# A decoder step with the memory keys at the head of its first portion and a gate bias added by VectorE

## The chip, the core and the metric

One core of a Trainium2 chip runs the kernel. The metric is the device time of one execution in microseconds (us). The runs of the kernel before took 2277.1, 2276.29 and 2273.66 us, so the median is 2276.29 us. Everything is float32.

## The reference, cut to what matters

Two layers, each over 256 prompt tokens (two tiles of 128) and 32 sample tokens, width 1024. What the first portion (layer 0, first prompt tile) has to compute, and where the change works:

```python
mem_n = _rmsnorm(mem_prompt, mem_norm_g[l])          # 256 memory tokens
kp = (mem_n @ w_mem_k[l]);  vp = (mem_n @ w_mem_v[l])  # keys and values, both outputs too
h = _rmsnorm(x, norm_mix_g) @ w_in                   # u_a v_a val_b gate_b q_m gl_a gl_b gl_m
s = einsum(tril(ws), layernorm(gelu(v_a))) + bs[:, :L]   # spatial gate, bias per group and token
y_a = gelu(u_a) * s
y_b = silu(layernorm(causal_depthwise(val_b * sigmoid(gate_b), w, b)))   # 31 taps
y_m = softmax(q_m @ kp * HD**-0.5) @ vp              # 4 heads of 256
x = x + (sig(gl_a)*(y_a@w_o_a) + sig(gl_b)*(y_b@w_o_b) + sig(gl_m)*(y_m@w_o_m)) @ w_out
x = x + peer(rmsnorm(x))     # 8 heads, 16 of 16384 experts each, rows fetched from memory
```

A norm of memory token t is a factor of t alone, and the gain a factor of the channel alone. So `mem_n @ W` can be had as `((gain * mem) @ W) * norm[t]`.

## The kernel before, in words

The work is cut into four portions m = 0 to 3: m = 0 and 2 are the first prompt tile of layer 0 and 1 (128 tokens), m = 1 and 3 the second tile with the 32 sample tokens. A portion's dense part is written out for each engine as a generator `mixing(m)`. Portion 0 runs by itself from the start of the kernel; the mixing of every later portion is woven into the expert stage of the portion before, by the tables `parts` and `PLACE`. The expert stage gathers pairs of expert rows with indirect DMAs and needs the scores that portion 0 ends with, so nothing of it runs before portion 0 is over.

Within portion 0 each engine takes its steps strictly in the order of the code. SP loads weights in pieces of 1024 KB into a ring of four buffers (`ring`, L400), in the order of `items(m)`; the load of piece n waits until TensorE has finished piece n-4. At the start SP first loads the token rows x, the constants, `small` (gains and taps) and `vecs`, then four ring pieces, then the memory (L418).

TensorE's pieces have short names. `glu0` to `glu7` are the conv module's gate and value, 16 matmuls of 128 columns each; `mk0` to `mk3` memory keys, 16 of 256 columns; `mv0` to `mv3` memory values, 16 of 256; `q0` to `q3` queries, 16 of 128; `va`, `ua` the spatial gate's v and u; `S`, `T`, `O` are scores, transposes and outputs of one attention head; `gt` and `pr` gate and own projections, 8 matmuls of 512 columns; `sg0` to `sg3` the spatial gate itself. A float32 matmul stands in the trace as two rows, so that a piece of 16 matmuls has x32. Its results go to three PSUM banks in turn (`dense`), and each piece waits until the result three pieces earlier has left its bank.

TensorE begins portion 0 by turning x (L1543, once VectorE has made the diagonal of row norms), then runs glu0 to glu7, mk0 with q0 and so on. The memory is normed in `ext_s` before mk0: ScalarE squares it, VectorE sums (L1021), takes the root's reciprocal and multiplies all eight blocks (L1030).

The depthwise convolution is VectorE's: 62 steps, each four instructions over a half of the channels and one tap (L962, L964). It can start when glu7 has left its bank. `beside(name, taps)` puts a fixed number of steps at a fixed place: 32 of them in the attention stretch, 8 before the first two `pr`, 16 among `ua` and `sg`. Whatever is left is done by `conv(2 * CONV_W)` after sg3. Then VectorE sums the blocks (L1225), TensorE adds over partitions (L1818, `csum`), and only behind that matmul do pr2 and the rest of portion 0 follow on TensorE.

In `spatial` each group's product gets the bias by a second, eight-row matmul (L1807), and VectorE multiplies the sum into u (L1221). With mv0 SP issues two spreads of LayerNorm vectors over all partitions (L446, 512 KB each, into `uv` buffers still free) and four early weight pieces for portion 1 (`EARLY`, L450, 1024 KB each).

Of the kernel before, what the change touches and what calls it, by code (L numbers as in the profile page):

```python
# [50 lines left out]
def items(m):  # L51
    if m % 2 == 0:
# [20 lines left out]
for _k, _c in WKIND:  # L73
# [8 lines left out]
    memsq=(1, 0), pe_memsq=(1, 0), memvar=(1, 0), rt_mem=(1, 0), memn=(8, 0), pe_mk=(4, 0), kt=(4, 0), pe_mv=(4, 0), vm=(4, 0),  # L82
# [28 lines left out]
def parts(p):  # L111
# [15 lines left out]
    out = [("rows", 4), ("tr", 6)] + some("glu", h, *range(8))  # L127
    if p == 0:
# [28 lines left out]
for _p in range(2):  # L157
    _at, _place = 0.0, {}
    for _name, _cost in parts(_p):
        _place[_name] = _at  # L160
        _at += _cost
    _place["end"] = _at
    PLACE.append(_place)
# [5 lines left out]
for _p in range(2):  # L169
# [4 lines left out]
def emptied(m, name):  # L174

    last = TURN[m % 2][name][1]
# [30 lines left out]
def build(nc, x_in, consts_in, mem_in, cache_in, state_in, w_in, small_in, vecs_in, fing_in, ws_in, wss_in,  # L207
          keys_in, uv_in, y_out, memk_out, memv_out, convp_out, convs_out, vn_out):
    with ExitStack() as ctx:
# [17 lines left out]
        spread_landed = sem("spread_landed")  # L227
        conv_stored, vn_stored, y_stored = sem("conv_stored"), sem("vn_stored"), sem("y_stored")
# [23 lines left out]
        ln_rows = [uvbuf[i][:, 0:D] for i in range(2)]  # L252

# [102 lines left out]
        def dense(m, name):  # L356
            return turn[TURN[m % 2][name][0] % 3]
# [13 lines left out]
        def _(sp):  # L371
            def load(m, kind, i):
                if (m, kind, i) in EARLY:
                    return
# [26 lines left out]

            sp.dma_start(x[:, 0], x_in[:, 0]).then_inc(x_landed[0], 16)
            sp.dma_start(consts[:, :], consts_in).then_inc(consts_landed, 16)
            for m in range(PORTIONS):
# [9 lines left out]
                for n, it in enumerate(items(m)):  # L414
                    if p == 0 and n == 4:
                        if m:
                            sp.wait_ge(S["pe_so"], at("pe_so", m, 0))
                        sp.dma_start(ext_s_flat[:, 0:KB * M], mem_in).then_inc(mem_landed, 16)  # L418
                        if m == 0:
# [63 lines left out]
        def _(pool):  # L483
# [27 lines left out]
            def mixing(m):  # L511
                l, p = m // 2, m % 2
                place = PLACE[p]
# [42 lines left out]
        def _(act):  # L556
# [18 lines left out]
            def mixing(m):  # L575
                l, p = m // 2, m % 2
                place, nt, tiles = PLACE[p], COLS[p], TB[p]

                yield place["rows"]
                if m != 1:  # L580
                    norm_rows(m)

                for c in range(KB):
# [8 lines left out]
                    if p == 0 and c == 1:  # L592
# [3 lines left out]
                    if p == 0 and c == (4 if m == 0 else 3):  # L596
# [67 lines left out]
                if p == 0:  # L664
# [268 lines left out]
        def _(dve):  # L933
            V = nc.vector

            def norm_rows(m):
                for i, t in enumerate(TB[m % 2]):
# [14 lines left out]
            def mixing(m):  # L952
                l, p = m // 2, m % 2
                place, nt, tiles = PLACE[p], COLS[p], TB[p]
# [45 lines left out]

                for c in range(KB):
# [17 lines left out]
                    if m == 0 and c == 2:  # L1019
                        dve.wait_ge(S["memsq"], 1)  # L1020
                        V.tensor_reduce(rb_mem, kT.rearrange("p c t -> p t c"), AX.X, ALU.add).then_inc(S["memred"], 1)  # L1021
                    if p == 0 and c == (4 if m == 0 else 2):
                        dve.wait_ge(S["pe_memsq"], at("pe_memsq", m, 1))
                        V.tensor_scalar(rb_mem, s_bank[0][:, 0:M], 1.0 / D, EPS, ALU.mult, ALU.add).then_inc(S["memvar"], 1)
                    if p == 0 and c == (5 if m == 0 else 4):
# [38 lines left out]
                if p == 0:  # L1064
# [114 lines left out]
                def norm_v_gain():  # L1179
# [5 lines left out]
                    if m == 0:  # L1185
                        dve.wait_ge(spread_landed, 32)
# [23 lines left out]
                def spatial():  # L1210
                    for i in range(3):
                        yield from beside(f"ua{i}", 2 - p)
                    for i in range(4):
# [6 lines left out]
                        u = yMA[:, 2 * i:2 * i + 2, 0:nt]  # L1220
                        V.tensor_tensor(u, u, two(dense(m, f"sg{i}"), nt), ALU.mult).then_inc(S["ya"], 1)  # L1221
# [218 lines left out]
            dve.wait_ge(consts_landed, 16)  # L1440
# [48 lines left out]
        def _(pe):  # L1489
# [627 lines left out]
```

## Time and profile before

| | |
|---|---|
| median of the runs | 2276.29 us |
| profiled execution, own time | 2276.56 us |
| its span | 2274.8 us |
| TensorE busy over the span | 71% |
| VectorE busy | 69% |
| ScalarE, GpSimd busy | 29% each |
| data moved | 895.53 MB, 394 GB/s on average |
| portion 0's dense part on TensorE | from 6.99 us to about 300 us |

The profiled execution's own time holds some 1.8 us outside its span. The shares are means over the whole kernel; the change touches only the first 200 us, and what counts there is which engine is waited for at which moment. The page's table in 40 slices shows TensorE at 8 to 9 tenths in the first slices of 57 us and the granted clock at 9 of 10 or more in the first seven.

### The profile page before, as it was taken

How to read it: one execution, taken by the hardware profiler on the slowest of the kernel's cores; microseconds unless marked ns; L12 is line 12 of the kernel's file. 1: busy time of each engine (PE TensorE's matmuls, PEld its weight loads, DVE VectorE, ACT ScalarE, POOL GpSimd, SP SyncE). 2: the span in 40 equal slices, each digit the busy share in tenths (PEclk: the TensorE clock that was granted, in tenths of full speed). 3: DMA queues.
4: the chain of work that ended last, by engine and by line, in shares of the span. 5: the costliest groups of instructions: out<-in, count | busy, mean ns of one | idle time of the engine just before them, and what ended most of it. 6: DMA issues, size and time to landing. Idle time of an engine off the chain costs nothing.

```text
span 2274.8 us, 31198 instructions
## 1 busy us (share of the span) xinstructions
PE 1623.5 (71%) x10876; PEld 1051.8 (46%) x10876; DVE 1576.3 (69%) x4199; ACT 662.8 (29%) x1662; POOL 662.1 (29%) x596
## 2 busy tenths in 40 slices
PE   8999977679898567778878656865999853334333
PEld 8865766347775235454533424632878620000001
DVE  3545277877767576877776557977776677776875
ACT  2112234321233232323123223342123333322222
POOL 0000032222233342323223233321223344444442
PEclk9999989779899678889979766986999875555555
DMA  8686789999999999999999999999999999999997
GB/s 305 262 301 240 288 332 422 419 421 422 412 408 419 421 420 421 422 397 419 421 394 415 421 421 403 422 403 421 382 420 421 418 398 422 422 422 421 421 421 308
DMA packets 127099, 895.53 MB, mean 394 GB/s; under 512 B 16064, under 2 KB 16896, under 8 KB 19168
## 3 DMA queue, kind: packets, MB, share of 16 engines
q0 software_dynamic: 83232, 604.02, 64.4%
q1 hardware_dynamic: 43712, 289.53, 31.8%
q8 instruction: 87, 1.43, 0.2%
q14 instruction: 68, 0.56, 0.1%
HBM read 885.38 MB, written 8.11 MB: 393 GB/s over the span
## 4 chain that ended last, share of the span: by engine, by line
PE 35%; DMA 34%; DVE 19%; issue 4%; ACT 4%; DVEq 3%; POOL 2%; another core or an unknown queue 0%; POOLq 0%; ACTq 0%
DMA uv<-uv_in,idx_u 24%; PE bank L1499 15%; DVE uv L1378 9%; PE bank L1754 5%; DMA ring<-w_in 5%; PE bank L1505 5%; PE bank L2006 4%; DMA ring<-cache_in 4%; DVE yB L964 2%; POOL uv L506 2%; ACT L558 1%; ACT diag L881 1%; DVE x L1399 1%; PE bank L1939 1%; DVEq L959 1%
## 5 line engine op out<-in xcount | busy, mean ns | idle before, releaser
L506 POOL DMA_INDIRECT uv<-uv_in,idx_u x574 | 645.9, 1125 | 1390.4 <-PE bank L2006 949.7
L1378 DVE CUSTOM_DVE_ANT_0 uv<-uv,xrep 128x1024 f32<-128x1024 f32 x576 | 683.3, 1224 | 219.5 <-DMA uv<-uv_in,idx_u 210.6
L2006 PE MATMUL bank<-uv,diag 128*32 128x512 f32 x2176 | 396.1, 809 | 456.4 <-ACT diag L881 445.8
L1499 PEld LDWEIGHTS bank<-xnT,ring 128*128 128x128 f32 x3200 | 434.6, 201 | 82.8 <-issue 67.0
L1499 PE MATMUL bank<-xnT,ring 128*128 128x160 f32 (+1 forms) x3200 | 456.2, 303 | 9.4 <-DMA ring<-w_in 7.7
L558 ACT ACTIVATE pick<-pick 128x2 f32<-128x2 f32 (+1 forms) x324 | 69.6, 215 | 1057.4 <-DVE pick L1378 1053.3
L2006 PEld LDWEIGHTS bank<-uv,diag 128*32 128x32 f32 x2176 | 50.1, 123 | 646.9 <-ACT diag L881 576.7
L964 DVE SCALAR_TENSOR_TENSOR yB<-ext_p,small,yB 128x128 f32<-128x128 f32 x960 | 275.6, 349 | 19.8 <-issue 0.3
L558 ACT ACT_TABLE_LOAD x140 | 179.6, 1283 | 2.4
L881 ACT ACTIVATE diag<-gated_fold,pick 128x32 f32<-128x32 f32 x576 | 153.6, 314 | 9.6 <-ACT pick L558 0.2
L1754 PE MATMUL bank<-ring,xnT 128*128 128x512 f32 x192 | 91.0, 631 | 0.0
L1499 PE MATMUL bank<-yMA,ring 128*128 128x160 f32 x512 | 74.8, 301 | 0.0
L558 ACT ACTIVATE phase<-bank 128x512 f32<-128x512 f32 (+2 forms) x44 | 23.2, 528 | 170.3 <-PE bank L1754 63.3
L1499 PEld LDWEIGHTS bank<-yMA,ring 128*128 128x128 f32 x512 | 71.8, 192 | 0.0
L865 ACT ACTIVATE xrep<-xnf 32x1024 f32<-32x1024 f32 x64 | 67.4, 1053 | 1.4
L1999 PE MATMUL bank<-uv,diag 128*32 128x256 f32 x256 | 30.9, 634 | 47.9 <-ACT diag L881 47.9
L1505 PE MATMUL bank<-ring,xnT 128*128 128x256 f32 x192 | 49.5, 418 | 20.9 <-DMA ring<-w_in 20.9
L558 ACT ACTIVATE sg<-bank 128x160 f32<-128x160 f32 (+1 forms) x80 | 23.4, 294 | 134.6 <-PE bank L1499 132.1
L1754 PEld LDWEIGHTS bank<-ring,xnT 128*128 128x128 f32 x192 | 38.1, 202 | 49.0 <-issue 48.5
L1505 PE MATMUL bank<-ring,ext_s 128*128 128x256 f32 x256 | 59.3, 392 | 0.0
L1754 PE MATMUL bank<-ring,yMA 128*128 128x512 f32 x128 | 58.3, 610 | 0.0
L1499 PE MATMUL bank<-ext_s,ring 128*128 128x256 f32 x256 | 57.0, 381 | 0.0
(228 smaller groups left out, 1771.8 us busy)
## 6 DMA issues: line engine op xcount, KB each, us to landing
ring<-w_in SPq DMA_DIRECT2D x216, 1024.0 KB
ring<-cache_in SPq DMA_DIRECT2D x32, 1024.0 KB
uv<-uv_in,idx_u POOLq DMA_INDIRECT x578, 12.8
uv<-w_in SPq DMA_DIRECT2D x4, 1024.0 KB, 13.3
ext_s<-state_in SPq DMA_DIRECT2D x2, 1088.0 KB, 13.1
convs_out<-ext_s SPq DMA_DIRECT2D x2, 1088.0 KB
ext_s<-mem_in SPq DMA_DIRECT2D x2, 1024.0 KB, 14.7
memk_out<-phase SPq DMA_DIRECT2D x2, 1024.0 KB, 11.7
```

The costliest lines, as they stand in the source:

```text
L506: nc.gpsimd.indirect_dma_start(out=uvbuf[2 * b + i], out_offset=None, in_=uv_in, in_offset=bass.IndirectOffsetOnAxis(ap=ids[:, c:c + 1], a ...
L558: ins = nc.scalar.activation(out, in_, func, bias=bias, scale=scale, **({} if accum is None else {"accum_out": accum}))
L865: ins = nc.scalar.activation(xrep[gg % 2][32 * i:32 * (i + 1), :], xnf[1 if t == 2 else 0][r0:r0 + 32], ACT.Copy)
L881: ins = nc.scalar.activation(diag[:, t % 4, i], gated_fold[:, c], ACT.Copy, scale=gel[:, 16 * (s % 2) + c:16 * (s % 2) + c + 1])
L959: dve.drain()
L964: ins = V.scalar_tensor_tensor(out=yB[:, c, 0:P], in0=ext_p[:, c, w:w + P], scalar=wconv[:, c, w:w + 1], in1=yB[:, c, 0:P], op0=ALU.mult, ...
L1378: ins = V.tensor_tensor_reduce(out=u, in0=u, in1=xrep[gg % 2][:, :], scale=1.0, scalar=0.0, op0=ALU.mult, op1=ALU.add, accum_out=hid[:, c: ...
L1499: ins = MM(out, w[:, k, P * b:P * (b + 1)], rhs(k), start=k == 0, stop=k == KB - 1)
L1505: ins = MM(out, lhs(k), w[:, k, :], start=k == 0, stop=k == KB - 1)
L1754: ins = MM(out[:, :], rows[:, 4 * (i % 2) + k, 0:P], w[:, k, :], start=i % 2 == 0 and k == 0, stop=i % 2 == 1 and k == 3)
L1999: ins = MM(vbank[gg % 2][32 * q:32 * (q + 1), 0:256], diag[:, t % 4, i], uvbuf[2 * b + i][:, c:c + 256], start=first and i == 0, stop=last ...
L2006: ins = MM(vbank[gg % 2][c:c + 32, :], diag[:, t % 4, i], uvbuf[2 * b + i][:, D + 512 * n:D + 512 * (n + 1)], start=first, stop=last)
```

## The change

It concerns portion 0 alone; the rows of portions 1 to 3 are the same instructions in the same order on every engine.

- SP first loads the memory gain alone (128 rows of 32 bytes), then the memory and the first key piece in halves of 512 KB each, in turns, then constants and x. The ring order becomes mk0 to mk3, glu0 to glu7, q0, q1, mv0, q2, mv1, q3, mv2, mv3, va.
- VectorE multiplies the eight memory blocks by the gain into a spare `uv` buffer (`memG`). TensorE makes the keys from that, before the norm is known. ScalarE and VectorE find the norm meanwhile, and VectorE multiplies the keys by it as they leave PSUM (`keys_of`); ScalarE did that copy before. The turning of x stands between mk1 and mk2. After glu1 VectorE makes the fully normed memory (eight multiplications) for the values.
- In the attention stretch mv pieces move ahead, between S and T of the heads. The steps of the convolution there are given out anew.
- The eight-row bias matmuls go from portion 0. SP spreads the bias over all partitions with a third DMA of 512 KB, and VectorE adds it (L1338 of the new kernel) into a spare buffer before it multiplies into u.

```diff
 def items(m):
-    if m % 2 == 0:
+    if m == 0:
+        kinds = [("mk", 0, 4), ("glu", 0, 8), ("q", 0, 2), ("mv", 0, 1), ("q", 2, 3), ("mv", 1, 2), ("q", 3, 4), ("mv", 2, 4), ("va", 0, 4)]
+    elif m % 2 == 0:
...
+            sp.dma_start(mem_gain[:, :], small_in[0:P, KB * (CONV_W + 1):KB * (CONV_W + 2)]).then_inc(gain_landed, 16)
+            first_piece = w_in[P * WROW["mk", 0]:P * (WROW["mk", 0] + 1), :]
+            sp.dma_start(ext_s_flat[:, 0:D], mem_in[:, 0:D]).then_inc(mem_first, 16)
+            sp.dma_start(ring[0][:, 0:D], first_piece[:, 0:D]).then_inc(first_landed, 16)
+            sp.dma_start(ext_s_flat[:, D:2 * D], mem_in[:, D:2 * D]).then_inc(mem_landed, 16)
+            sp.dma_start(ring[0][:, D:2 * D], first_piece[:, D:2 * D]).then_inc(w_landed[0], 16)
+            sp.dma_start(consts[:, :], consts_in).then_inc(consts_landed, 16)
             sp.dma_start(x[:, 0], x_in[:, 0]).then_inc(x_landed[0], 16)
-            sp.dma_start(consts[:, :], consts_in).then_inc(consts_landed, 16)
...
-                        for i, rows in enumerate((LN_G, LN_B)):
-                            sp.dma_start(ln_rows[i], vecs_in[rows, :]...
+                        for to, rows in ((ln_rows[0], LN_G), (ln_rows[1], LN_B), (bs_rows, BS)):
+                            sp.dma_start(to, vecs_in[rows, :]...
...
+                def keys_of(i):
+                    dve.wait_ge(S["pe_mk"], i + 1)
...
+                    V.tensor_tensor(kT[:, 2 * i:2 * i + 2], two(dense(m, f"mk{i}"), M), rb_mem.unsqueeze(1).to_broadcast([P, 2, M]),
+                                    ALU.mult).then_inc(S["kt"], 1)
                 yield place["rows"]
+                if m == 0:
...
+                        V.tensor_scalar(memG[:, k], memT[:, k], mem_gain[:, k:k + 1], None, ALU.mult).then_inc(S["memg"], 1)
+                    dve.wait_ge(S["memsq"], 1)
+                    V.tensor_reduce(rb_mem, mem_squares.rearrange("p (c t) -> p t c", c=KB), AX.X, ALU.add).then_inc(S["memred"], 1)
...
+                if m == 0:
+                    yield from beside("q0", 2)
+                    yield from beside("q1", 2)
+                    yield from att_max(0)
+                    yield from beside("mv0", 3)
+                    att_norm(0)
+                    yield from att_max(1)
+                    yield from beside("q2", 3)
+                    att_norm(1)
+                    yield from beside("mv1", 3)
+                    yield from att_max(2)
+                    yield from beside("q3", 2)
+                    att_norm(2)
+                    yield from beside("mv2", 3)
+                    yield from att_max(3)
+                    yield from beside("mv3", 2)
+                    att_norm(3)
+                    yield from beside("va0", 2)
+                    yield from beside("va1", 2)
+                    yield from beside("va2", 2)
...
-                        u = yMA[:, 2 * i:2 * i + 2, 0:nt]
-                        V.tensor_tensor(u, u, two(dense(m, f"sg{i}"), nt), ALU.mult).then_inc(S["ya"], 1)
+                        u, got = yMA[:, 2 * i:2 * i + 2, 0:nt], two(dense(m, f"sg{i}"), nt)
+                        if m == 0:
+                            V.tensor_tensor(biased, got, bs_rows[:, 256 * i:256 * (i + 1)].rearrange("p (b t) -> p b t", b=2), ALU.add)
+                            dve.drain()
+                            got = biased
+                        V.tensor_tensor(u, u, got, ALU.mult).then_inc(S["ya"], 1)
...
+                if m == 0:
+                    yield from first_keys()
+                    yield from mk(1)
+                    yield from turn_first()
+                    yield from mk(2)
+                    yield from mk(3)
+                for c in range(KB):
+                    yield from glu(c)
+                if m == 0:
+                    yield from q(0)
+                    yield from q(1)
+                    yield from att_scores(0)
+                    yield from mv(0)
+                    yield from att_scores(1)
+                    yield from att_turn(0)
+                    yield from q(2)
+                    yield from mv(1)
...
-                        MM(out[:, a:a + P], vn[0][:, ch], wsT[:, g], start=True, stop=False)
-                        ins = MM(out[:, a:a + P], row_g, vecs[BS, :], start=False, stop=True)
+                        ins = MM(out[:, a:a + P], vn[0][:, ch], wsT[:, g], start=True, stop=m == 0)
+                        if m:
+                            ins = MM(out[:, a:a + P], row_g, vecs[BS, :], start=False, stop=True)
```

TensorE at the head of the program, before. L1543 turns x, and each pair of L1499 rows (one and 15) is one glu piece:

```order
L1543 MATMUL bank<-sg,x 128x128 [waits s_xrow,consts_landed]
L1543 MATMUL bank<-sg,x 128x128 x7
L1499 MATMUL bank<-xnT,ring 128x128 [waits w_landed0,s_xnt]
L1499 MATMUL bank<-xnT,ring 128x128 x15
L1499 MATMUL bank<-xnT,ring 128x128 [waits w_landed1]
L1499 MATMUL bank<-xnT,ring 128x128 x15
L1499 MATMUL bank<-xnT,ring 128x128 [waits w_landed2]
```

And in the changed kernel. L1703 is mk0 from the gained memory (`uv`), L1707 the sum of squares over partitions, L1618 with `uv` a later key piece, L1667 the turning of x:

```order
L1703 MATMUL bank<-uv,ring 128x256 [waits s_memg,first_landed]
L1703 MATMUL bank<-uv,ring 128x256 [waits s_memg] x3
L1703 MATMUL bank<-uv,ring 128x256 x4
L1703 MATMUL bank<-uv,ring 128x256 [waits s_memg,w_landed0]
L1703 MATMUL bank<-uv,ring 128x256 [waits s_memg] x3
L1703 MATMUL bank<-uv,ring 128x256 x4
L1707 MATMUL bank<-merged,consts 128x256 [waits s_memred,consts_landed]
L1618 MATMUL bank<-uv,ring 128x256 [waits w_landed1]
L1618 MATMUL bank<-uv,ring 128x256 x15
L1667 MATMUL bank<-sg,x 128x128 [waits s_xrow]
L1667 MATMUL bank<-sg,x 128x128 x7
L1618 MATMUL bank<-uv,ring 128x256 [waits w_landed2]
```

The keys stand where the turning of x stood, and the turning comes behind mk1.

SP's queue around the spreads, before. L400 loads a ring piece and names the engine it waits for, L446 the spreads, L450 the early pieces; the row behind them is the load of q3:

```order
L400 DMA ring<-w_in 128x2048 [waits s_pe_glu] x8
L400 DMA ring<-w_in 128x2048 [waits s_pe_mk]
L400 DMA ring<-w_in 128x2048 [waits s_pe_q]
L400 DMA ring<-w_in 128x2048 [waits s_pe_mk]
L400 DMA ring<-w_in 128x2048 [waits s_pe_q]
L446 DMA uv<-vecs_in 128x1024 x2
L450 DMA uv<-w_in 128x2048 x4
L400 DMA ring<-w_in 128x2048 [waits s_pe_mk]
L400 DMA ring<-w_in 128x2048 [waits s_pe_q]
```

And in the changed kernel, where L473 are the spreads and L477 the early pieces; the last of the seven loads ahead of them is mv0, and the row behind the early pieces is the load of q2:

```order
L421 DMA ring<-w_in 128x2048 [waits s_pe_mk] x4
L421 DMA ring<-w_in 128x2048 [waits s_pe_glu] x7
L473 DMA uv<-vecs_in 128x1024 x3
L477 DMA uv<-w_in 128x2048 x4
L421 DMA ring<-w_in 128x2048 [waits s_pe_glu]
L421 DMA ring<-w_in 128x2048 [waits s_pe_q] x2
```

One more spread is ahead of the load behind them, and that load is now q2's.

VectorE at the end of the spatial gate, before. L964 are conv steps (four rows each), L1221 the multiplication into u for sg2 and sg3, L1225 the sum that `csum` waits for:

```order
L964 SCALAR_TENSOR_TENSOR yB<-ext_p,small,yB 128x128 x8
L1221 TENSOR_TENSOR yMA<-yMA,bank 128x2x128 [waits s_ua,s_pe_sgu]
L964 SCALAR_TENSOR_TENSOR yB<-ext_p,small,yB 128x128 x8
L1221 TENSOR_TENSOR yMA<-yMA,bank 128x2x128 [waits s_ua,s_pe_sgu]
L964 SCALAR_TENSOR_TENSOR yB<-ext_p,small,yB 128x128 x24
L1225 TENSOR_REDUCE rb<-yB 128x128
```

And in the changed kernel, where L1338 is the added bias and L1341 the multiplication:

```order
L1029 SCALAR_TENSOR_TENSOR yB<-ext_p,small,yB 128x128 x8
L1338 TENSOR_TENSOR uv<-bank,uv 128x256 [waits s_ua,s_pe_sgu]
L1341 TENSOR_TENSOR yMA<-yMA,uv 128x2x128
L1029 SCALAR_TENSOR_TENSOR yB<-ext_p,small,yB 128x128 x8
L1338 TENSOR_TENSOR uv<-bank,uv 128x256 [waits s_ua,s_pe_sgu]
L1341 TENSOR_TENSOR yMA<-yMA,uv 128x2x128
L1029 SCALAR_TENSOR_TENSOR yB<-ext_p,small,yB 128x128 x48
L1345 TENSOR_REDUCE rb<-yB 128x128
```

Behind sg3 stand 48 conv instructions instead of 24, and each multiplication has an addition ahead of it.

## Rows read from the trace of the kernel before

**Rows 1.** Windows: length, busy PE, PEld, DVE, ACT, POOL, then clock, DMA share, GB/s.
```profile
20.00:30.00 10.00, 10.00 (x90) 9.95 (x89) 4.12 (x3) 2.84 (x7) 0.00 (x0) 1.00 1.00 383
```

**Rows 2.** Timeline of TensorE, 0 to 60 us: start, us, engine, line.
```profile
6.99 3.65 PE L1543 MATMUL bank<-sg,x 128*128 128x128 f32 x16 [6.99 <-DVE sg L948]
11.42 18.13 PE L1499 MATMUL bank<-xnT,ring 128*128 128x128 f32 x160 [0.78 <-DVE xnT L994]
...
40.54 7.07 PE L1499 MATMUL bank<-ext_s,ring 128*128 128x256 f32 x32
47.45 3.73 PE L1499 MATMUL bank<-xnT,ring 128*128 128x128 f32 x32
```

**Rows 3.** Groups, 0 to 200 us: busy us, mean ns, idle before with releaser.
```profile
L1627 PE MATMUL bank<-merged,phase 128*128 128x128 f32 x32 | 4.4, 282 | 2.2 <-issue 2.2
```

**Rows 4.** The chain of waits at the start: when, how long, what.
```profile
0.82 3.79 DMA x<-x_in
```

**Rows 5.** Timeline at the start: SP's issue, ScalarE's squares, VectorE's sum.
```profile
4.59 1.21 SPq L418 DMA_DIRECT2D ext_s<-mem_in  x1
...
19.40 1.89 ACT L558 ACTIVATE phase<-ext_s 128x2048 f32<-128x2048 f32 x1
...
23.37 3.72 DVE L1021 TENSOR_REDUCE merged<-phase 128x256 f32<-128x2048 f32 x1
```

**Rows 6.** DMA issues, 4 to 4.6 us: size, us to landing.
```profile
ext_s<-mem_in SPq DMA_DIRECT2D x1, 1024.0 KB, 14.7
```

**Rows 7.** Timeline of SP's issues around the spreads.
```profile
62.56 0.33 SPq L400 DMA_DIRECT2D ring<-w_in  x1
...
62.93 0.91 SPq L446 DMA_DIRECT2D uv<-vecs_in  x2
...
63.88 2.15 SPq L450 DMA_DIRECT2D uv<-w_in  x4
```

**Rows 8.** DMA issues: first spread; median of both; third and fourth early piece.
```profile
uv<-vecs_in SPq DMA_DIRECT2D x1, 512.0 KB, 5.7
...
uv<-vecs_in SPq DMA_DIRECT2D x2, 512.0 KB, 6.6
...
uv<-w_in SPq DMA_DIRECT2D x1, 1024.0 KB, 14.3
...
uv<-w_in SPq DMA_DIRECT2D x1, 1024.0 KB, 16.3
```

**Rows 9.** Timeline of TensorE, 170 to 212 us.
```profile
190.00 0.48 PE L1807 MATMUL bank<-vecs,consts 8*128 8x128 f32 x2
190.42 7.13 PE L1754 MATMUL bank<-ring,xnT 128*128 128x512 f32 x16
200.27 0.49 PE L1818 MATMUL bank<-rb,consts 128*128 128x128 f32 x2 [2.72 <-DVE rb L1225]
200.60 8.73 PE L1754 MATMUL bank<-ring,yMA 128*128 128x512 f32 x16
```

**Rows 10.** Timeline of VectorE, 174 to 206 us.
```profile
190.53 0.42 DVE L1221 TENSOR_TENSOR yMA<-yMA,bank 128x256 f32<-128x256 f32 x1 [4.55 <-PE bank L1807]
191.04 7.21 DVE L964 SCALAR_TENSOR_TENSOR yB<-ext_p,small,yB 128x128 f32<-128x128 f32 x24
198.34 1.88 DVE L1225 TENSOR_REDUCE rb<-yB 128x128 f32<-128x1024 f32 x1
```

**Rows 11.** Windows of TensorE's clock, columns as in rows 1.
```profile
7.00:8.00 1.00, 1.00 (x5) 1.00 (x6) 0.00 (x0) 0.58 (x1) 0.00 (x0) 1.00 1.03 434
88.00:90.00 2.00, 1.27 (x7) 0.84 (x6) 0.00 (x0) 0.97 (x3) 0.00 (x0) 1.00 0.83 340
202.00:203.00 1.00, 1.00 (x2) 0.33 (x1) 0.02 (x1) 0.94 (x1) 0.00 (x0) 0.50 0.00 0
...
263.00:264.00 1.00, 0.73 (x4) 0.76 (x5) 0.79 (x2) 0.00 (x0) 0.00 (x0) 0.50 1.05 434
268.00:269.00 1.00, 1.00 (x6) 1.00 (x6) 0.00 (x0) 0.00 (x0) 0.00 (x0) 0.50 0.02 9
```

More of the change, by code:

```diff
@@ L106, in freed, with part_of, parts @@
     return name, at(name, m, k)
-def parts(p):
+def part_of(m):
+    return 2 if m == 0 else m % 2
+def parts(part):
+    p = part % 2
     h, across = (3.6, 4.4)[p], (3.5, 4.8)[p]
@@ L125, in O @@
         return some("O", 1.2, i)
-    out = [("rows", 4), ("tr", 6)] + some("glu", h, *range(8))
-    if p == 0:
+    out = [("rows", 4)] + (some("mk", kv, 0, 1) if part == 2 else []) + [("tr", 6)] + (some("mk", kv, 2, 3) if part == 2 else [])
+    out += some("glu", h, *range(8))
+    if part == 2:
+        out += some("q", h, 0, 1) + S(0) + some("mv", kv, 0) + S(1) + T(0) + some("q", h, 2) + some("mv", kv, 1) + S(2) + T(1) + O(0)
+        out += some("q", h, 3) + some("mv", kv, 2) + S(3) + T(2) + O(1) + some("mv", kv, 3) + T(3) + O(2)
+        out += some("va", across, 0, 1) + O(3) + some("va", across, 2, 3)
+    elif p == 0:
         out += some("mk", kv, 0) + some("q", h, 0) + some("mk", kv, 1) + S(0) + some("q", h, 1) + some("mk", kv, 2) + S(1) + T(0)
@@ L156 @@
 PLACE = []
-for _p in range(2):
+for _p in range(3):
     _at, _place = 0.0, {}
@@ L168 @@
 TURN = []
-for _p in range(2):
+for _p in range(3):
     _names = [_n for _n, _ in parts(_p) if _n.rstrip("0123456789") in DENSE]
@@ L512, in mixing @@
                 l, p = m // 2, m % 2
-                place = PLACE[p]
+                place = PLACE[part_of(m)]
                 yield place["tr"]
@@ L595, in mixing @@
                         A(kT, memT, ACT.Square, "memsq")
-                    if p == 0 and c == (4 if m == 0 else 3):
+                    if m == 2 and c == 3:
                         act.wait_ge(S["memvar"], at("memvar", m, 1))
@@ L1553, in bank_for, with glu @@
                     return dense(m, name)
-                for c in range(KB):
+                def glu(c):
                     yield place[f"glu{c}"]
@@ L1569, in mixing, with first_keys @@
                         ins.then_inc(S["pe_memsq"], 1)
+                def first_keys():
+                    yield place["mk0"]
+                    w, out = buf(0, "mk", 0).rearrange("p (k c) -> p k c", k=KB), dense(0, "mk0")
+                    for half in range(2):
+                        if half:
+                            pe.wait_ge(*landed(0, "mk", 0))
+                        else:
+                            pe.wait_ge(first_landed, 16)
+                        for b in range(2):
+                            for k in range(4 * half, 4 * half + 4):
+                                if b == 0:
+                                    pe.wait_ge(S["memg"], k + 1)
+                                ins = MM((out, s_bank[1])[b][:, 0:M], w[:, k, P * b:P * (b + 1)], memG[:, k], start=k == 0, stop=k == KB - 1)
+                    ins.then_inc(S["pe_mk"], 1)
+                    pe.wait_ge(consts_landed, 16)
+                    pe.wait_ge(S["memred"], 1)
+                    MM(s_bank[0][:, 0:M], ones, rb_mem, start=True, stop=True).then_inc(S["pe_memsq"], 1)
                 def mk(i):
                     yield place[f"mk{i}"]
-                    if i == 0:
+                    if m and i == 0:
                         pe.wait_ge(S["memn"], at("memn", m, 8))
-                    w, out = weights(m, "mk", i), bank_for(f"mk{i}")
+                    w, out, mem = weights(m, "mk", i), bank_for(f"mk{i}"), memT if m else memG
                     for b in range(2):
-                        ins = down(out[:, 256 * b:256 * (b + 1)], w, b, lambda k: memT[:, k])
+                        ins = down(out[:, 256 * b:256 * (b + 1)], w, b, lambda k: mem[:, k])
                     ins.then_inc(S["pe_mk"], 1)
```

141 lines of the change are left out of this document (110 added, 31 removed).

## The prediction

> **What bounds the kernel now.** I read the windows first. In portion 0 TensorE is busy in all of a stretch of 10 us at a granted clock of 1.00 while VectorE is busy in 4 of 10 [rows 1]. So up to 190 us TensorE's own list of work is the path, and what counts there is when it starts, what is on the list, and each pause. TensorE's timeline gives the start: its first matmul at 6.99 us, a pause of 0.78 us before glu0 at 11.42, a key piece in 6.91 us (40.54 to 47.45), and a glu piece, as long as a query piece, in 18.13 / 5 = 3.6 [rows 2]. The grouped view gives the pauses in the attention stretch: 2.2 us in all ahead of L1627, where an output matmul stands right behind the mv piece whose copy to `phase` it needs [rows 3]. At the end of the spatial gate it turns over: TensorE waits 2.72 us for the sum over blocks before `csum` at 200.27 [rows 9], and VectorE had been at its last conv steps since 191.04 [rows 10]. There VectorE is the path. Portion 0 ends in the scores that the expert stage needs, so I take a microsecond at `csum` as a microsecond of the whole.
>
> **Term 1, start and pauses: -3.4 us.** Before, TensorE waits for x (landed at 0.82 + 3.79 = 4.6 us) [rows 4] and the chain of its norm. After, it waits for half the memory and half a key piece. The queue's pace: the memory of before was issued at 4.59 and took 14.7 us [rows 5, 6], so it landed at 19.3, with some 5350 KB (the rest of the constants and vectors, four ring pieces, itself) behind x; that is 2.75 us per 1024 KB. The first 1024 KB of the new order then are there at 4.6 + 0.5 x 2.75 = 6.0, plus 0.45 for one more issue ahead of them and a little for the small rows of the gain: 6.6 us. The second halves, at about 9.2, come before the first half of mk0 is through. So the start is 0.4 us earlier (6.99 - 6.6), the pause of 0.78 goes, and the 2.2 us go because in the new list S and T stand between mv and O: 3.4 us. The list itself is equally long up to the spatial gate.
> What hides the norm: the squares take 1.89 us and the sum 3.72 [rows 5]; from the memory's landing at about 8.0 the sum is there at 13.7. TensorE is through mk0 only at 6.6 + 6.91 and the 1.8 us of the next paragraph, 15.3, so the wait for it is over by then. The rest (root, reciprocal, the keys' multiplication, x's diagonal) runs under mk1 until 22 us. mk1's weights, 3850 KB down the queue, land at about 14.3, one microsecond ahead of need. The eight multiplications for the values run on VectorE beside the glu pieces, where it idles. If the first bytes come at 6.0 or at 7.5, the term is -4.0 or -2.5.
> The turning of x took 3.65 us for 16 rows of 128 columns, 0.228 us each, the glu rows behind it 18.13 for 160, 0.113 each [rows 2]: at first TensorE runs at half pace, which costs 1.8 us. I let the keys pay the same 1.8, so it drops out. The clock column shows 1.00 there [rows 11], and by that column alone the keys would run at full pace from the first, since nothing else halves them; the term would be -5.2. The Trainium skill, "TensorE: Matmul & The Clock Gate", section on the HAM clock gate, says that throttled is the default state and activity releases it. By that rule any first piece pays, and the trace's durations agree with it, its clock column does not. By the column the whole sum would be +4.6, by the rule +6.4.
>
> **Term 2, a new wait for q2: +3.0 us.** The order of SP's queue puts three spreads and four early pieces (5632 KB) between the loads of mv0 and q2, where two spreads and the same pieces stood ahead of q3. Before, mv0 was issued at 62.56 [rows 7]. The fourth early piece, issued at 65.6, took 16.3 us and landed at 81.9, the third, issued at 65.0, at 79.3 [rows 7, 8]: 2.5 us per 1024 KB. The load behind them is there between 82.3 (its bytes partly in flight with theirs) and 84.4. The first spread landed at 62.93 + 5.7 = 68.6 and the second, by the pair's median of 6.6, at about 70.9, so a further one costs 1.3 (its bytes) to 2.3 us. After, then, q2 is there 21.0 to 24.1 us after the issue of mv0. That issue follows the end of glu6. From there TensorE has glu7, q0, q1 (3 x 3.6), mv0 (6.9), and two S and a T (10 trace rows at a piece's 0.2 each, 2.0): 19.7 us. The wait is 1.3 to 4.4 us; I take 3.0, above the middle, since the early pieces' spacing speaks for a queue in order.  Behind q2 stand mv1 and all of attention on TensorE. mv1 lands 2.5 us behind q2, whose work takes 3.6: no second wait.
>
> **Term 3, the clock after that wait: +1.6 us.** After the pause of 2.72 us pr2 took 8.73 us for 16 rows, gt3 before it 7.13 [rows 9], with the clock at 0.50 [rows 11]: 1.6 us lost. The pauses of 0.73 us left it at 1.00 [rows 11]. Bounds: nothing, and 3.0 (elsewhere it stood at 0.50 at 263 and still at 268 us [rows 11], some 6 us, half of them lost).
>
> **Term 4, the end of the spatial gate: +4.4 us.** The bias matmuls go: each held TensorE for 0.42 us (190.00 to 190.42) [rows 9], eight of them 3.3 us. That is all on TensorE's path up to sg3. VectorE has 4.55 us of idle before sg3's product [rows 10], so the additions (0.5 us each, the multiplication's 0.42 and a drain) for sg0 to sg2 are hidden: 1.5 + 3.3 of these 4.55 are used up, so that VectorE is 0 to 0.3 us late. At sg3 the addition is on the path, +0.5. Then the conv steps: the new placing has 2+2+3+3+3+2+3+2+2+2+2 = 26 in the attention stretch for 32, the places behind are unchanged, so 12 stand behind sg3 instead of 6 (48 instructions for 24 in the order). 24 took 7.21 us [rows 10], so six steps more are +7.2. Nothing hides them: TensorE has only gt3 (7.13 us) behind sg3 and waits already. -3.3 + 0.5 + 7.2 = +4.4 us at `csum`; its bounds are 4.2 and 4.7. TensorE's pause before `csum` grows from 2.7 to about 10.7 us.
>
> **Term 5, the clock at csum: +0.8 us.** It falls already before and costs 1.6. After a pause four times as long TensorE starts slow instead of falling slow after a microsecond; bounds 0 and 1.4 (3.0 - 1.6).
>
> Other edits cost nothing: ScalarE loses the key copies; GpSimd has the same list; the third spread is awaited only at the LayerNorm gain, some 60 us behind its landing.
>
> **Sum.** -3.4 + 3.0 + 1.6 + 4.4 + 0.8 = +6.4 us. Against the profiled execution's own 2276.56 (span 2274.8 and 1.8 around it) that is 2283.0. This execution stands 0.3 above the median of 2276.29, so the forecast for the median is 2282.7 us, 0.28% slower.
>
> **Rivals.**
> 1. q2 is there in time. Its load is not strictly last (the windows leave room for a microsecond or two), the third spread costs its bytes only, and the clock stays up. Terms 2 and 3 go: +1.8 us, 2278.1, and 2276 if the keys also start at full pace. For it: rows show no TensorE wait for a ring piece in this stretch before. Against: the early pieces' landings 2.5 us apart.
> 2. Longer half-clock stretches at both pauses and the longest wait: -2.5 + 4.4 + 3.0 + 4.7 + 1.4 = +11.0, 2287.3.
> 3. Faster: the tail of the convolution is covered, so that TensorE's list alone counts. Then -3.4 - 3.3 = -6.7, 2269.6, if q2 is in time too. It decides from the point where 0.5 + 12 steps + the sum of 1.88 us end within gt3's 7.13, that is 0.40 us a step. The measured step is 1.20, its first six in nothing slower than before; I see no cover.
> 4. By the clock column (above): +4.6, 2280.9; it belongs to the forecast's own range.
>
> **How the numbers follow.** Forecast with its bounds 0.55, rival 1 0.29, rival 2 0.08, rival 3 and whatever else helps 0.08. About 0.2%, 4.6 us, is what can be told from no change here. Of the forecast's 0.55, 0.10 lies inside it. So faster 0.08, within 0.39 (0.29 + 0.10), slower 0.53. The range goes from 2274.5 (below rival 1 by the spread of the runs) to 2288.5 (rival 2 and a little).
>
> **What would show it.** TensorE's first matmul at 6.6 us and mk1 without a wait: term 1. A pause of TensorE ahead of q2, released by the DMA of the ring, with a clock of 0.50 behind it: terms 2 and 3; no pause there is rival 1. 48 conv instructions in about 14.4 us behind sg3, `csum` released by VectorE after a pause of some 10 us and at about 206 to 208 us: term 4. If TensorE waited for the sum of squares or mk1's weights, the start would be wrong. If `csum` comes before 200.3, rival 3 holds.

## The result and the profile after

The changed kernel takes 2285.96 us (median of 5 runs, 2284.88 to 2288.05) against 2276.8 for the kernel before (5 runs, 2273.66 to 2277.21). The ratio is 1.0039, 95% interval 1.0028 to 1.005: 9.2 us slower. Forecast were 2282.7 us, a range of 2274.5 to 2288.5, and slower by more than 0.2% with a chance of 0.53. The direction was right and the size was forecast at 6.4 instead of 9.2.

The profiled execution has a span of 2283.0 us (2274.8 before). (The page of the kernel before has the granted clock at 9 tenths in the first five slices and in the seventh but at 8 in the sixth, in which portion 0 ends; it is not at 9 in all of the first seven.) TensorE's timeline of the first 256 us, in the same columns as [rows 2, 9]:

```profile
7.99 9.04 PE L1703 MATMUL bank<-uv,ring 128*128 128x256 f32 x32 [7.99 <-DMA ring<-w_in]
16.87 0.59 PE L1707 MATMUL bank<-merged,consts 128*128 128x256 f32 x2
17.30 7.07 PE L1618 MATMUL bank<-uv,ring 128*128 128x256 f32 x32
24.20 1.95 PE L1667 MATMUL bank<-sg,x 128*128 128x128 f32 x16
...
84.17 0.38 PE L1753 MATMUL bank<-consts,merged 128*128 128x128 f32 x2
89.34 5.92 PE L1618 MATMUL bank<-xnT,ring 128*128 128x128 f32 x32 [4.78 <-DMA ring<-w_in]
...
103.08 1.06 PE L1767 MATMUL bank<-merged,phase 128*128 128x128 f32 x8
103.97 3.74 PE L1618 MATMUL bank<-xnT,ring 128*128 128x128 f32 x32
...
139.16 7.03 PE L1927 MATMUL bank<-ring,xnT 128*128 128x512 f32 x16
...
189.13 0.61 PE L1979 MATMUL bank<-phase 128*128 128x128 f32 x4
189.57 7.03 PE L1927 MATMUL bank<-ring,xnT 128*128 128x512 f32 x16
208.15 0.80 PE L1992 MATMUL bank<-rb,consts 128*128 128x128 f32 x2 [11.54 <-DVE rb L1345]
208.74 9.25 PE L1927 MATMUL bank<-ring,yMA 128*128 128x512 f32 x16
218.04 7.03 PE L1927 MATMUL bank<-ring,yMA 128*128 128x512 f32 x16
```

Three things stand out. The keys start at 7.99, released by the DMA of the first piece. Ahead of q2, at 89.34, TensorE idles 4.78 us and is released by the ring's DMA; q2 then takes 5.92 us where q3 behind it takes 3.74. Ahead of `csum` it idles 11.54 us (2.72 before [rows 9]), and pr2 behind it takes 9.25 us against 7.03.

For the middle of the account, gt0 and pr3 of the kernel before, from its TensorE timelines:

```profile
135.25 7.03 PE L1754 MATMUL bank<-ring,xnT 128*128 128x512 f32 x16
...
209.38 7.03 PE L1754 MATMUL bank<-ring,yMA 128*128 128x512 f32 x16
```

gt0 comes 3.91 us later than there (139.16 - 135.25), `csum` 7.88 later (208.15 - 200.27). The turning of x for portion 1, right behind portion 0's last matmul pieces, started at 284.00 before and at 292.45 after, 8.45 us later. The span is 8.2 us longer. pr3 had come 8.66 later (218.04 - 209.38). So what was lost by 218 us is the whole of the difference, to within half a microsecond, as assumed. VectorE after, beside [rows 10]:

```profile
190.62 0.42 DVE L1338 TENSOR_TENSOR uv<-bank,uv 128x256 f32<-128x256 f32 x1
191.11 0.43 DVE L1341 TENSOR_TENSOR yMA<-yMA,uv 128x256 f32<-128x256 f32 x1
191.63 14.49 DVE L1029 SCALAR_TENSOR_TENSOR yB<-ext_p,small,yB 128x128 f32<-128x128 f32 x48
206.21 1.88 DVE L1345 TENSOR_REDUCE rb<-yB 128x128 f32<-128x1024 f32 x1
```

48 conv instructions in 14.49 us for 24 in 7.21. The addition at sg3 has no idle ahead of it, so VectorE was late there. The clock columns of two stretches (columns as in [rows 1]):

```profile
92.00:93.00 1.00, 1.00 (x7) 1.00 (x6) 0.85 (x4) 0.00 (x0) 0.00 (x0) 0.50 0.94 393
94.00:95.00 1.00, 1.00 (x12) 1.00 (x11) 0.00 (x0) 0.00 (x0) 0.00 (x0) 1.00 1.03 434
...
207.00:208.00 1.00, 0.00 (x0) 0.00 (x0) 1.00 (x1) 0.00 (x0) 0.00 (x0) 0.50 0.00 0
209.00:210.00 1.00, 1.00 (x2) 0.41 (x2) 1.00 (x1) 0.00 (x0) 0.00 (x0) 0.50 0.00 0
```

Granted is 0.50, the lower level of 1.2 GHz, behind each of the two pauses, and 1.00 (2.4 GHz) at 94 us. Rows of 128 columns that touch the microsecond are 7 at 92 us and 12 at 94. Ahead of `csum` it stands at 0.50 already inside the pause (207 us), where TensorE does nothing.

### The profile page after: what moved, and what is told of

Read it like the earlier page. It is cut to its first block, busy times and chain, and to the rows that moved or that the text cites. A ratio compares the mean times of both kernels' runs of the same rounds, so it can differ in the third digit from the quotient of the medians.

```text
span 2283.0 us, 31187 instructions
## 1 busy us (share of the span) xinstructions
PE 1625.4 (71%) x10860; PEld 1054.9 (46%) x10860; DVE 1584.8 (69%) x4216; ACT 657.7 (29%) x1656; POOL 670.0 (29%) x596
## 4 chain that ended last, share of the span: by engine, by line
DMA 36%; PE 33%; DVE 18%; ACT 4%; issue 4%; DVEq 3%; POOL 2%; SPq 0%; another core or an unknown queue 0%; POOLq 0%; ACTq 0%
DMA uv<-uv_in,idx_u 26%; PE bank L1618 15%; DVE uv L1498 8%; DMA ring<-w_in 6%; PE bank L2180 5%; PE bank L1927 4%; PE bank L1624 4%; DMA ring<-cache_in 4%; DVE yB L1029 3%; POOL uv L533 2%; ACT L585 1%; DVE x L1519 1%; ACT diag L944 1%; DVEq L1024 1%; PE bank L2113 1%
## 5 line engine op out<-in xcount | busy, mean ns | idle before, releaser
L533 POOL DMA_INDIRECT uv<-uv_in,idx_u x574 | 654.1, 1139 | 1382.9 <-PE bank L2180 947.1
L1618 PEld LDWEIGHTS bank<-xnT,ring 128*128 128x128 f32 x3200 | 437.4, 202 | 84.5 <-issue 67.1
L1618 PE MATMUL bank<-xnT,ring 128*128 128x160 f32 (+1 forms) x3200 | 458.7, 304 | 10.9 <-DMA ring<-w_in 10.2
L1927 PE MATMUL bank<-ring,xnT 128*128 128x512 f32 x192 | 86.8, 607 | 0.0
L1618 PE MATMUL bank<-yMA,ring 128*128 128x160 f32 x512 | 74.2, 299 | 0.0
L1618 PEld LDWEIGHTS bank<-yMA,ring 128*128 128x128 f32 x512 | 71.2, 190 | 0.0
L1624 PEld LDWEIGHTS bank<-ring,ext_s 128*128 128x128 f32 x256 | 50.5, 199 | 8.8 <-issue 1.7
```

What stands on the lines that cost most here:

```text
L533: nc.gpsimd.indirect_dma_start(out=uvbuf[2 * b + i], out_offset=None, in_=uv_in, in_offset=bass.IndirectOffsetOnAxis(ap=ids[:, c:c + 1], a ...
L1618: ins = MM(out, w[:, k, P * b:P * (b + 1)], rhs(k), start=k == 0, stop=k == KB - 1)
L1624: ins = MM(out, lhs(k), w[:, k, :], start=k == 0, stop=k == KB - 1)
L1927: ins = MM(out[:, :], rows[:, 4 * (i % 2) + k, 0:P], w[:, k, :], start=i % 2 == 0 and k == 0, stop=i % 2 == 1 and k == 3)
```

## The experiments

The runs of e1 to e4 shared one set of runs of the kernel before (median 2278.59), those of e5 to e8 another (2269.86), so they are compared by their ratio to it; 0.1% is 2.3 us. The intervals of the ratios are 0.1% or so to either side, hence a difference of two ratios is good to some 3 to 4 us, and smaller ones rest on the traces, one per kernel.

**e1, no conv step behind sg3.** The counts of `beside` in the changed kernel's attention stretch:

```diff
-q0 2  q1 2  mv0 3  q2 3  mv1 3  q3 2  mv2 3  mv3 2  va0 2  va1 2  va2 2   (26)
+q0 2  q1 3  mv0 5  q2 3  mv1 5  q3 3  mv2 5  mv3 4  va0 3  va1 3  va2 2   (38)
```

> The changed kernel with 38 conv steps in the attention stretch instead of 26, so that none is left behind sg3. My theory (the tail of the convolution is on the path, its pause costs the clock too): the pause of 11.5 us ahead of csum goes altogether, since gt3 (7.03 us) covers the last addition, the multiplication and the sum over blocks; the half-clock stretch behind it (2.2 us) goes as well. 2286.0 - 11.5 - 2.2 = about 2272.3. The wait of 4.8 us for q2 stays. Rival (VectorE's idle time in the attention stretch is not free: more steps there delay the softmax and so TensorE): new pauses ahead of T0 or T1, and a time above 2276. Rival 2 (the loss is in the start and the wait, the tail is hidden elsewhere): 2284 or more.

Measured: 0.9978 (0.9969 to 0.9987), from 1.0039; that is -0.61%, 13.9 us, as expected (13.7). Its TensorE timeline:

```profile
89.86 6.75 PE L1618 MATMUL bank<-xnT,ring 128*128 128x128 f32 x32 [4.00 <-DMA ring<-w_in]
...
190.94 7.03 PE L1927 MATMUL bank<-ring,xnT 128*128 128x512 f32 x16
198.03 7.03 PE L1927 MATMUL bank<-ring,yMA 128*128 128x512 f32 x16
205.12 7.03 PE L1927 MATMUL bank<-ring,yMA 128*128 128x512 f32 x16
```

gt3, pr2 and pr3 follow each other 7.09 us apart, `csum` and `csq` in between without a pause, and no softmax is late. The wait for q2 is still there. So the tail of the convolution and its clock cost are worth 13 to 14 us in the changed kernel (pr3 comes at 205.12 instead of 218.04), and VectorE's idle time in the attention stretch could hold the steps. Both rivals fall.

**e2, spreads and early pieces later in SP's queue.**

```diff
-                    if m == 0 and (kind, i) == ("mv", 0):
+                    if m == 0 and (kind, i) == ("q", 3):
```

> The changed kernel with the three spreads and four early pieces issued behind the load of q3 instead of behind that of mv0. My theory (q2's load stands behind 5632 KB in SP's queue): the wait of 4.8 us ahead of q2 and its half-clock stretch (2.2 us) go, mv2 is needed late enough. 2286.0 - 7.0 = 2279.0. Rival (the DMA engines are simply too slow for the new order in this stretch, whatever stands first): the wait moves to mv2 or mv3 and the time stays within 2 us of 2286.

Measured: 1.0002 (0.9993 to 1.0011), -0.37% or 8.4 us against the changed kernel's ratio; expected were 7.0, and the span of its trace is 6.5 shorter. One row of its TensorE timeline shows all that is left of the wait in the whole attention stretch, another the pause ahead of `csum`:

```profile
101.00 7.17 PE L1624 MATMUL bank<-ring,ext_s 128*128 128x256 f32 x32 [0.41 <-DMA ring<-w_in]
...
132.72 7.03 PE L1927 MATMUL bank<-ring,xnT 128*128 128x512 f32 x16
...
201.70 0.80 PE L1992 MATMUL bank<-rb,consts 128*128 128x128 f32 x2 [11.54 <-DVE rb L1345]
```

0.41 us moved to mv2, not 4.78. gt0 comes at 132.72, 6.4 us earlier than in the changed kernel, and the 11.54 ahead of `csum` are untouched. It was the place in the queue, not the DMA engines' pace.

**e3, keys first without the bias part.** Changed kernel, two spreads, eight-row matmuls back:

```diff
-                        for to, rows in ((ln_rows[0], LN_G), (ln_rows[1], LN_B), (bs_rows, BS)):
+                        for to, rows in ((ln_rows[0], LN_G), (ln_rows[1], LN_B)):
...
-                        if m == 0:
+                        if False:
                             V.tensor_tensor(biased, got, bs_rows[:, ...
...
-                        ins = MM(out[:, a:a + P], vn[0][:, ch], wsT[:, g], start=True, stop=m == 0)
-                        if m:
-                            ins = MM(out[:, a:a + P], row_g, vecs[BS, :], start=False, stop=True)
+                        ins = MM(out[:, a:a + P], vn[0][:, ch], wsT[:, g], start=True, stop=False)
+                        ins = MM(out[:, a:a + P], row_g, vecs[BS, :], start=False, stop=True)
```

> The changed kernel with the bias part undone: two spreads, the eight-row matmuls back, no addition on VectorE; keys first as changed. My theory: q2's wait shrinks by the third spread (2.7 us) to about 2 and its clock cost a little; at the spatial gate csum comes 3.5 us later relative to gt0 (TensorE's sg pieces 5.0 longer, of which VectorE had left 1.0 unused, less the addition's 0.5). Together about 2286. Rival (the bias part is what costs, by its DMA and VectorE's additions; the keys gain): 2278 or below.

Measured: 1.0036 (1.0022 to 1.0049), the same as the changed kernel within the intervals. TensorE:

```profile
86.79 3.84 PE L1618 MATMUL bank<-xnT,ring 128*128 128x128 f32 x32 [2.26 <-DMA ring<-w_in]
...
188.15 0.39 PE L1979 MATMUL bank<-phase 128*128 128x128 f32 x2
...
189.71 7.13 PE L1927 MATMUL bank<-ring,xnT 128*128 128x512 f32 x16
206.85 0.80 PE L1991 MATMUL bank<-rb,consts 128*128 128x128 f32 x2 [10.00 <-DVE rb L1345]
```

With two spreads the wait for q2 is 2.26 us and in this execution costs no clock (3.84 for q2, granted clock 1.00). Against the changed kernel's trace the third spread makes 2.5 of the 4.78; against the waits with three spreads in e1 and e7, 4.00 and 5.92, it would be 1.7 and 3.7. An sg piece with its bias matmuls takes 1.56 us (188.15 to 189.71), without them 0.44 (189.13 to 189.57 above). What the bias part costs at q2 it mostly gives back at the spatial gate: gt0 comes at 134.54 here and at 139.16 with it, 4.6 us for wait and clock, and from gt0 to `csum` it is 72.3 us here and 69.0 with it, 3.3 us back.

**e4, the bias part alone, on the kernel before.** The same two edits as in the change (third spread, addition on VectorE, no eight-row matmul when m is 0), nothing of the keys.

> The kernel before with the bias part alone: third spread, additions on VectorE, no eight-row matmuls. My theory: the third spread is hidden, since the load behind it (q3's) has 6 us of slack; sg3's product leaves its bank 4.0 us earlier as in the changed kernel, the addition takes 0.5: csum 3.5 us earlier, 2276.8 - 3.5 = 2273.3. Rival (the bias part costs): 2278 to 2281.

Measured: 0.9983 (0.9974 to 0.9992), 3.9 us faster; expected were 3.5. In its trace gt0 starts at 137.06 and `csum` at 198.40, 61.3 us apart instead of 65.0. (gt0 itself is 1.8 us later than before because the slow stretch at the start was longer in this execution: the first 160 rows of the glu pieces took 19.96 us instead of 18.13.)

```profile
137.06 7.03 PE L1760 MATMUL bank<-ring,xnT 128*128 128x512 f32 x16
...
198.40 0.49 PE L1825 MATMUL bank<-rb,consts 128*128 128x128 f32 x2 [3.90 <-DVE rb L1231]
```

No wait for the ring appears in the attention stretch. Where the load behind the spreads has slack, the bias part gains.

**e5, both remedies together.** The edits of e1 and e2 in the changed kernel.

> The changed kernel with both edits of e1 and e2: 38 conv steps in the attention stretch, spreads and early pieces behind the load of q3. My theory: the two losses are independent, each a pause of TensorE with its clock cost, so the gains add: 2286.0 - 13.7 - 7.0 = 2265.3, a ratio to the kernel before of 0.995. Rival (they share something: with the wait for q2 gone VectorE has less time in the attention stretch, so its 38 steps hold up the softmax or csum): 2268 to 2272, with pauses ahead of T or csum.

Measured: 0.9941 (0.9928 to 0.9954), 13.4 us faster than the kernel before; a ratio of 0.995 was expected. TensorE has no pause between its first matmul and 231 us:

```profile
8.25 8.55 PE L1703 MATMUL bank<-uv,ring 128*128 128x256 f32 x32 [8.25 <-DMA ring<-w_in]
...
131.81 7.03 PE L1927 MATMUL bank<-ring,xnT 128*128 128x512 f32 x16
...
189.09 0.39 PE L1992 MATMUL bank<-rb,consts 128*128 128x128 f32 x2
```

The two losses add up as independent ones do: 0.61 + 0.37 = 0.98%, measured 1.0039 to 0.9941, also 0.98%. The rival falls.

**e6, the gain's load third.** e5 with

```diff
-            sp.dma_start(mem_gain[:, :], ...).then_inc(gain_landed, 16)
             first_piece = ...
             sp.dma_start(ext_s_flat[:, 0:D], mem_in[:, 0:D]).then_inc(mem_first, 16)
             sp.dma_start(ring[0][:, 0:D], first_piece[:, 0:D]).then_inc(first_landed, 16)
+            sp.dma_start(mem_gain[:, :], ...).then_inc(gain_landed, 16)
```

> As e5, but the load of the memory gain (128 rows of 32 bytes) is issued third, behind the first halves of memory and key piece, instead of first. It tells why TensorE's start came at 8.0 us and not at 6.6. Theory A (the small rows at the head of the queue hold up what is behind them): the first halves land 0.5 to 1.4 us earlier, the gain is there by then, start at 7 us, 2264.5. Theory B (half pieces, with rows of 4 KB out of rows of 8 KB, move more slowly than whole ones, the gain's place is nothing): start at 7.5 to 8.5 us, time as e5.

Measured: 0.9943 (0.993 to 0.9956), no difference from e5.

```profile
7.56 9.19 PE L1703 MATMUL bank<-uv,ring 128*128 128x256 f32 x32 [7.56 <-DVE uv L1069]
16.59 0.59 PE L1707 MATMUL bank<-merged,consts 128*128 128x256 f32 x2
```

And its DMA rows for the first key half (issued at 1.28 us) and, of e5, the same (issued at 1.74), us to landing last:

```profile
ring<-w_in SPq DMA_DIRECT2D x1, 512.0 KB, 5.6
```

```profile
ring<-w_in SPq DMA_DIRECT2D x1, 512.0 KB, 6.5
```

The half lands at 6.9 instead of 8.2 us, and in the six traces with the gain first it lands between 7.9 and 8.4. So the small rows at the head did hold it up, by 1.4 us against e5, where one issue takes 0.46 (theory A for the landing). Now the gain is late: it lands at 7.03, VectorE multiplies by it, and TensorE starts at 7.56 instead of 8.25. L1707 behind mk0 starts at 16.59 against 16.64 in e5, since mk0 took 9.19 us for 8.55. Whether the earlier start made its slow stretch longer is not shown: with the gain first mk0 took 8.55 to 9.99 us from execution to execution. Nor can times with intervals of 3 us to either side tell a gain of 0.7. So theory A held for the landing, and what it is worth stays open.

**e7, matmuls in the pause.**

```diff
                     if m == 0:
+                        for _ in range(46):
+                            MM(t_bank[:, 0:P], ones, ident, start=True, stop=True)
                         pe.wait_ge(S["cred"], 1)
```

> The changed kernel with 46 matmuls of 128 columns on constants, into a bank that is free, in the pause ahead of csum; their results are used by nobody. They take some 10 of the pause's 11.5 us. Theory (the pause's second price is the clock: csum and pr2 run at half pace for 5 us behind it): pr2 back to 7.0 us, csum's moment unchanged, 2286.0 - 2.2 = 2283.8. Rival (the slow stretch has another cause, such as VectorE's and ScalarE's traffic at that moment): pr2 stays at 9 us, 2286.

Measured: 1.0026 (1.0017 to 1.0036), 3.0 us below the changed kernel's ratio (2.2 expected), with intervals that overlap.

```profile
90.63 5.24 PE L1618 MATMUL bank<-xnT,ring 128*128 128x128 f32 x32 [5.92 <-DMA ring<-w_in]
...
197.06 10.44 PE L1992 MATMUL bank<-consts 128*128 128x128 f32 x92
208.77 0.49 PE L1994 MATMUL bank<-rb,consts 128*128 128x128 f32 x2 [1.27 <-DVE rb L1345]
209.09 7.03 PE L1927 MATMUL bank<-ring,yMA 128*128 128x512 f32 x16
```

```profile
210.00:211.00 1.00, 1.00 (x4) 0.52 (x3) 0.52 (x1) 0.45 (x1) 0.00 (x0) 1.00 0.00 0
```

pr2 takes 7.03 us again, at a granted clock of 1.00 (last line, columns as in [rows 1]), with the same VectorE and ScalarE work beside it. From `csum` to pr3 it is 7.41 us (216.18 - 208.77) instead of 9.89. The slow pr2 was the clock. The trace shows it; the times alone would not.

**e8, the conv steps re-placed without the keys first.** e4 with 38 conv steps in the attention stretch (one more beside mk3, mv0, mv1 and mv3, two more beside mv2).

> The kernel before (keys behind the glu pieces) with the bias part of the change and 38 conv steps in the attention stretch instead of 32: what the first portion gives without the keys at its head. Theory: 3.9 us (e4) and the pause ahead of csum (3.9 us in e4) with its clock cost (1.7): 2276.8 - 9.5 = 2267.3, a ratio of 0.9958; the keys at the head are then worth only the 2 to 3 us between this and e5. Rival (the keys at the head are what makes room for the steps): pauses in the attention stretch, 2271 or more.

Measured: 0.9955 (0.9943 to 0.9968), expected 0.9958. No pause stands ahead of its `csum`:

```profile
185.87 7.03 PE L1760 MATMUL bank<-ring,xnT 128*128 128x512 f32 x16
192.74 0.39 PE L1825 MATMUL bank<-rb,consts 128*128 128x128 f32 x2
```

0.9955 to e5's 0.9941: keys first and the new order of the attention stretch together are worth 0.14%, 3.2 us, about term 1, though the intervals overlap. In the traces `csum` comes at 192.74 here and at 189.09 in e5. So 10.2 of e5's 13.4 us come from the bias part and the conv steps, with the keys where they were. The two halves of the new order, keys at the head and mv between S and T, were never run apart; what each is worth is read from rows only, under term 1.

## Why the prediction was right, and where it fell short

| term | forecast | measured | from |
|---|---|---|---|
| 1 start and pauses | -3.4 | -3.1 | gt0 +3.91, less terms 2 and 3 |
| 2 wait for q2 | +3.0 | +4.8 | 4.78 ahead of q2 |
| 3 clock behind it | +1.6 | +2.2 | q2 5.92 against 3.74 |
| 4 end of the spatial gate | +4.4 | +4.0 | `csum` +7.88, less gt0's +3.91 |
| 5 clock at `csum` | +0.8 | +0.8 | `csum` to pr3: 9.89 us (218.04 - 208.15) against 9.11 (209.38 - 200.27) |
| sum | +6.4 | +8.7 | |

The measured sum is how much later pr3 starts. The span grew by 8.2, the two profiled executions' own times differ by 8.5 and the medians by 9.2. The mechanism was right in every term; the term that was mis-sized is term 2, and term 1 and term 4 came out near by errors that cancel.

**Term 1.** The start was too early: forecast 6.6, measured 7.99. The step that failed is the queue's pace, taken as a single number from a landing 14.7 us long (which by the forecast's own figures, 14.7 us for 5350 KB, is 2.8 us per 1024 KB and not 2.75, a trifle). The first half key piece took 6.2 us from its issue at 1.74:

```profile
1.74 6.20 DMA ring<-w_in
```

e6 shows that the small load of the gain ahead of it had a part of that. The rest stays open: halves of a piece were not tried against whole ones. So the start came 1.0 us later than before and not 0.4 earlier, 1.4 us worse than forecast, and yet the term came out only 0.3 worse. That is luck. The pauses in the attention stretch were worth more than the 2.2 us of idle time in [rows 3]. Before:

```profile
81.92 7.07 PE L1505 MATMUL bank<-ring,ext_s 128*128 128x256 f32 x32
89.73 1.13 PE L1627 MATMUL bank<-merged,phase 128*128 128x128 f32 x8 [0.73 <-issue]
90.69 3.74 PE L1499 MATMUL bank<-xnT,ring 128*128 128x128 f32 x32
```

The mv piece with its output took 8.77 us there (81.92 to 90.69). The same two take 6.91 and 0.89 (103.08 to 103.97), 7.8, in the new order. Three times that is 2.9 us, and a pause of 0.26 us ahead of one S at 94.90, which the forecast left out, brought 0.5 more with the rows around it. Together that is 3.4 for the forecast's 2.2.

The norm was hidden as forecast: mk1 follows L1707 at 17.30 without a wait. mk0 paid 2.0 us for its slow start (9.04 against mk1's 7.07) where the turning of x had paid 1.7 (3.65 against 1.95 now); forecast was 1.8 for both. In that stretch the clock column reads 1.00:

```profile
10.00:11.00 1.00, 1.00 (x4) 0.82 (x3) 0.40 (x2) 1.00 (x1) 0.00 (x0) 1.00 1.00 398
13.00:14.00 1.00, 1.00 (x6) 0.90 (x5) 1.00 (x1) 0.42 (x2) 0.00 (x0) 1.00 1.03 426
```

By the rule of the Trainium skill, "TensorE: Matmul & The Clock Gate", section on the HAM clock gate, that the throttled state is the default, the trace agrees in its durations and not in its column; rival 4 falls.

**Term 2** was mis-sized: +4.8 for +3.0, just above the bound of 4.4. The mechanism was right (e2). q2's load landed 24.3 us after the issue of mv0 (89.29 - 65.01), forecast 21.0 to 24.1. The step that failed is the price of a further spread, 1.3 to 2.3 us, taken from the landing of the second one. The third is dearer. The second and third spread of the changed kernel were issued at 65.86 and 66.33:

```profile
uv<-vecs_in SPq DMA_DIRECT2D x1, 512.0 KB, 8.2
...
uv<-vecs_in SPq DMA_DIRECT2D x1, 512.0 KB, 10.5
```

They landed at 74.1 and 76.8, 2.8 us apart; in e1, e4 and e7 it is 2.3, 2.9 and 3.9. The other part is that I took 3.0 inside 1.3 to 4.4, whose lower end let q2's bytes be in flight beside those of the early pieces. The chain of waits shows the load's 20 us in the queue:

```profile
69.06 20.23 DMA ring<-w_in
```

It landed at 89.29, 2.5 us behind the fourth early piece (86.8): the queue served it last. Rival 1 (no wait) falls by every trace with the changed queue; with three spreads the waits are 4.00, 4.78 and 5.92 us.

**Term 3** is +2.2 for +1.6, inside its bounds, and the largest uncertainty from execution to execution: behind a wait for q2 the 32 rows took 5.92, 6.75 (e1), 5.24 (e7) and 3.84 us (e3, wait of 2.26). The longest wait, e7's 5.92, did not cost the most.

**Term 4** was near in sum, with two errors that cancel. The bias matmuls were worth 4.76 us on TensorE, not 3.3: from gt0 to gt3 it has 50.41 us instead of 55.17. The product's own rows take 0.11 us each without an eight-row matmul between them, and some 0.2 with it. But VectorE could not use all of it; it was 1.0 us late at sg3, since its four steps between sg0 and sg1 and the additions filled its time. -4.76 + 1.0 + 0.5 + 7.28 = +4.0. Rival 3, the covered tail, falls: the steps took 1.21 us each. e1 shows what a tail that is out of the way is worth.

**Term 5** was right in size and in its way: before, the clock still read 1.00 at 200 us, with `csum` and the first rows of pr2, and fell behind them; now it reads 0.50 ahead of `csum`. e7 shows the whole price by filling the pause and leaving VectorE's work: 2.5 us from `csum` to pr3, for the forecast's 1.6 + 0.8.

## What to carry to other kernels

When an order written by hand is changed, count what each other engine is given per place, not only the pieces that move: here a better order for TensorE left VectorE six conv steps short, and 5.6 MB of queue entries in front of a load that was now needed sooner. An idle engine upstream (VectorE in the attention stretch) is where such a remainder belongs. A gain that is argued on TensorE's list is worth only what the engine that is waited for can take of it (the bias matmuls' 4.8 us on TensorE moved VectorE's work on sg3 by 3.8). And a new pause can have a second price, the clock behind it: here the pauses of 2.7 us and more ahead of q2 and `csum` did, those of 0.73, 1.27 (e7) and 2.26 us (e3) did not.

## What the runs showed of the hardware

- Removing a matmul of eight rows from between matmuls of 128 rows saved more than its own time: an sg piece went from 1.56 to 0.44 us, 0.20 to 0.11 us a row. Eight of them had 3.3 us of their own and their going saved 4.76 from gt0 to gt3; with them back (e3) gt0 to gt3 is 55.17 us again.
- A spread of 4 KB over 128 partitions (512 KB written) took more of the queue than its bytes: the second landed 1.3 to 2.3 us behind the first and the third 2.3 to 3.9 behind the second, where early pieces of 1024 KB landed 2.4 to 2.5 apart in the changed kernel's trace.
- A load of 128 rows of 32 bytes at the head of the queue held back the 512 KB of the key piece behind it by 1.1 to 1.5 us with its issue of 0.46 (landing at 6.9 us in e6, at 7.9 to 8.4 in the six traces with the small load first).
- The clock column read 1.00 at the start of every execution while the rows took twice their time, until 11 to 16 us (the longest in e4). Behind the pauses of 2.72 us and more ahead of q2 and `csum` it read 0.50, and the rows agreed.
- TensorE's slow stretch at the start differs between executions: with the gain's load first mk0 took from 8.55 to 9.99 us. With the gain third (e6) TensorE started 0.7 us earlier than in e5 and was through mk0 at the same moment, in one trace.
